# Latents projected by features, sums of squares by matmul, queries rotated on VectorE, and retention's chunks four slots apart

## The chip, the cores and the metric

The kernel runs on one core of a Trainium2 chip, as one program. The metric is the device time of one execution in microseconds. Where a text says TensorE, VectorE, ScalarE, GpSimd and SyncE, the profile writes PE (PEld for its weight loads), DVE, ACT, POOL and SP.

## The reference

A model of two layers on 1024 tokens of width 1024. Each layer projects `h` to 3,120 columns, runs four mixers on slices of them, joins them by `w_out`, and adds a feed-forward part. What the change touches, cut to it:

```python
(ssm_z, ssm_xbc, ssm_dt, mla_cq, mla_ckv, mla_kr, ret_q, ret_k, ret_v, ret_g,
 nsa_q, nsa_kc, nsa_vc, nsa_ks, nsa_vs, nsa_kw, nsa_vw, nsa_gate) = split_columns(h @ w_in[l])
y_b = mla(mla_cq, mla_ckv, mla_kr, ...)
# mla: latents of 256 and 128, a shared rope key of 32, 4 heads of 64 + 32
q = (rms_norm(c_q, q_norm_g) @ w_uq).reshape(bsz, S, H, 96)
q = concat([q_nope, apply_rope(q_pe, cos, sin)]) * 96 ** -0.5
kv = (rms_norm(c_kv, kv_norm_g) @ w_ukv).reshape(bsz, S, H, 64 + 64)
k = concat([k_nope, broadcast(apply_rope(k_rope, cos, sin))])
# rms_norm: x * rsqrt(mean(x * x) + 1e-5) * g;  apply_rope: [x1 cos - x2 sin, x1 sin + x2 cos]
# retention: chunks of 128 tokens, one after the other through a state
```

Everything is float32. The kernel gets this precision in the large products with pairs of a high and a low part and three matmuls for each product.

## The kernel before

Tokens are tiled by 128 (`NT` = 8 tiles). `hybrid_layers` calls for each layer `mixers`, `attention` and `dense`. In each of them every engine has its own program, written out by hand in order, and waits for the others by semaphores; `phase` ends a block with a barrier of all engines. SyncE issues all transfers. `ahead` is one tile with one semaphore through which a block's last act loads the first data of the next.

`mixers` projects the columns group by group (`projection_groups`, line 903). A group has its weights loaded by SyncE (`load`), split into a high part by ScalarE (`split_hi`, line 1286) and a low part by GpSimd (`low`, line 1085), one group ahead of its use. TensorE works by slots: a token group of n columns has 8 units, one for each tile, of 24 matmuls with the tile as weights and n columns moving (`tokens_unit`, lines 1115 to 1117). A group by features has 4 units, of 24 matmuls with 128 columns of the weights stationary and 512 tokens moving, each cut over two slots (`projected_features`, lines 1131 to 1133). ScalarE takes each unit from PSUM into `stage` (`take`, lines 1318 and 1320), and after each half of a group SyncE stores it to DRAM: `proj` and `tok` by tokens, `proj_T` by features (`store`). Between the slots TensorE gets the small matmuls of the state space (a chunk each 4 slots) and then of retention: chunk t starts at slot 33 + 5t of the 72, with parts j = 0 to 3 in four successive slots, and its output is scaled on VectorE at j = 4 (line 1593). VectorE rotates the chunk's queries and keys two slots ahead (`rotate`, lines 1548 to 1560). The groups after retention's are: two of 208 columns by tokens (cq, ckv, kr), nq and kc+vc+ks+kw of 256 by features, and vs+vw+gate of 140 by tokens. The block's end loads half of the latents.

`attention` has two blocks. The first (lines 1677 to 1878) makes the MLA queries, keys and values: TensorE turns a tile's latents (`turn`, line 1766), VectorE scales them by the gains into `cT` (`copy_c`, line 1844), TensorE projects them up (lines 1791 to 1793, fp32, two instructions a matmul), ScalarE squares the latents with an accumulator (`square`, lines 1805, 1806), VectorE and GpSimd make the root of the mean (lines 1836, 1752), and ScalarE and VectorE take the products scaled by it (`take`, lines 1811 and 1812; `values`, line 1853). GpSimd rotates queries and keys a half (4 tiles) at a time (`rotate`, lines 1734 to 1743). Then TensorE turns queries and keys tile by tile into the one buffer `pT` (`turn_qk`, lines 1774 and 1779), and ScalarE and VectorE split them into high and low parts (`highs`, `lows`, lines 1816 to 1860). The second block computes maxima, scores and sums.

## Time and profile before

| | us |
|---|---|
| time of three runs: lowest, median, highest | 3117.3, 3121.11, 3121.22 |
| the profiled execution | 3122.69 |
| its span in the trace | 3120.9 |
| TensorE busy in it | 2939.0 |

The profile is of one execution. The span is the time from its first to its last recorded instruction; the rest of the execution's time lies around it. Times in the rows are microseconds from the span's start, "mean ns" is nanoseconds. A timeline row reads: start, duration, engine, line, instruction, output <- inputs, and in brackets the idle time before it and what ended it. Matmuls overlap, so the distance between two starts is their price, not the duration of one. "x2" on a row means that so many instructions were merged in it.

### The profile page before, as it was taken

To read this page: it belongs to the slowest core of one execution; us is meant where nothing else is said; L and a number is where in the kernel's file an instruction comes from. 1 tells how busy PE (TensorE), PEld (TensorE's weight loads), DVE (VectorE), ACT (ScalarE), POOL (GpSimd) and SP (SyncE) were. 2 spreads that over 40 slices of the span, in tenths; PEclk is the share of its full clock that TensorE was granted. 3 is DMA by queue.
4 is the path that set the end of the run, shared out by engine and by line. 5 is a ranking of instruction groups with operands and counts; after the bars stand their busy time and mean duration, and the time that the engine had idled before them with its cause. 6 is when DMAs were issued, how large, how long until landed. Compare 5 with 4: busy or idle time off the path is not lost. (4 is left out here: it accounts for less than half of the span.)

```text
span 3120.9 us, 38057 instructions
## 1 busy us (share of the span) xinstructions
PE 2939.0 (94%) x15186; PEld 2372.2 (76%) x15186; DVE 1522.1 (49%) x2571; ACT 818.5 (26%) x1375; POOL 320.4 (10%) x284
## 2 busy tenths in 40 slices
PE   4999978999999999999979999799999999999997
PEld 4899855656878888888768998466567888888885
DVE  5554434354644444444645533434555444444456
ACT  3322132434221121122223221234342211112111
POOL 4121132000000000000221212320000000000003
PEclk9999987999999999999989999689999999999998
DMA  4123314103011111011121232321030110111111
GB/s 160 54 62 89 92 56 85 41 1 109 27 64 45 54 55 54 28 53 55 54 78 34 73 108 75 84 51 28 1 135 28 54 54 33 49 54 54 54 41 54
DMA packets 143190, 186.00 MB, mean 60 GB/s; under 512 B 29072, under 2 KB 118800, under 8 KB 143016
## 3 DMA queue, kind: packets, MB, share of 16 engines
q1 hardware_dynamic: 143016, 183.57, 19.2%
q8 instruction: 122, 2.00, 0.3%
q14 instruction: 52, 0.43, 0.0%
HBM read 153.83 MB, written 29.72 MB: 59 GB/s over the span
## 5 line engine op out<-in xcount | busy, mean ns | idle before, releaser
L691 PE MATMUL dense_acc<-mlp_w2hi,mlp_ahi 128*128 128x512 f32 x1024 | 400.3, 391 | 4.2 <-DVE mlp_alo L823 4.2
L387 PE MATMUL dense_tr<-x_hi,mlp_w1hi 128*128 128x512 f32 x1024 | 400.5, 391 | 3.8 <-PEq L474 3.8
L832 DVE TENSOR_TENSOR h<-h,dense_acc 128x512 f32<-128x512 f32 x448 | 302.1, 686 | 204.1 <-PE dense_acc L693 204.1
L389 PE MATMUL dense_tr<-x_hi,mlp_w1lo 128*128 128x512 f32 x1024 | 400.0, 391 | 0.0
L388 PE MATMUL dense_tr<-x_lo,mlp_w1hi 128*128 128x512 f32 x1024 | 399.9, 391 | 0.0
L693 PE MATMUL dense_acc<-mlp_w2hi,mlp_alo 128*128 128x512 f32 x1024 | 399.8, 390 | 0.0
L692 PE MATMUL dense_acc<-mlp_w2lo,mlp_ahi 128*128 128x512 f32 x1024 | 399.4, 390 | 0.0
L1115 PE MATMUL mix_acc<-mix_whi,x_hi 128*128 128x256 f32 (+3 forms) x1024 | 294.4, 287 | 13.4 <-DVE mix_wlo L1410 13.4
L817 DVE TENSOR_TENSOR mlp_square<-mlp_square 128x512 f32<-128x512 f32 x128 | 88.4, 692 | 440.4 <-ACT mlp_square L757 440.4
L1116 PE MATMUL mix_acc<-mix_wlo,x_hi 128*128 128x256 f32 (+3 forms) x1024 | 287.4, 281 | 0.0
L1117 PE MATMUL mix_acc<-mix_whi,x_lo 128*128 128x256 f32 (+3 forms) x1024 | 286.7, 280 | 0.0
L691 PEld LDWEIGHTS dense_acc<-mlp_w2hi,mlp_ahi 128*128 128x128 f32 x1024 | 193.1, 189 | 45.3 <-issue 5.4
L387 PEld LDWEIGHTS dense_tr<-x_hi,mlp_w1hi 128*128 128x128 f32 x1024 | 193.3, 189 | 44.2 <-issue 4.2
L2247 ACT ACTIVATE att_PT<-att_ST 128x512 f32<-128x512 f32 (+2 forms) x244 | 135.2, 555 | 340.3 <-PE att_ST L2140 205.5
L389 PEld LDWEIGHTS dense_tr<-x_hi,mlp_w1lo 128*128 128x128 f32 x1024 | 193.2, 189 | 40.2
L388 PEld LDWEIGHTS dense_tr<-x_lo,mlp_w1hi 128*128 128x128 f32 x1024 | 193.2, 189 | 40.1
L692 PEld LDWEIGHTS dense_acc<-mlp_w2lo,mlp_ahi 128*128 128x128 f32 x1024 | 193.1, 189 | 40.1
L693 PEld LDWEIGHTS dense_acc<-mlp_w2hi,mlp_alo 128*128 128x128 f32 x1024 | 192.8, 188 | 40.3
L1115 PEld LDWEIGHTS mix_acc<-mix_whi,x_hi 128*128 128x128 f32 x1024 | 196.5, 192 | 14.5 <-DVE mix_wlo L1410 14.2
L757 ACT ACTIVATE mlp_square<-dense_tr 128x512 f32<-128x512 f32 x128 | 76.3, 598 | 481.4 <-PE dense_tr L389 479.2
L749 ACT ACTIVATE mlp_w2hi<-mlp_raw 128x2048 fp32r<-128x2048 f32 x32 | 61.3, 1916 | 535.3 <-PE dense_acc L693 535.3
L1116 PEld LDWEIGHTS mix_acc<-mix_wlo,x_hi 128*128 128x128 f32 x1024 | 196.4, 192 | 0.1
(306 smaller groups left out, 5022.3 us busy)
## 6 DMA issues: line engine op xcount, KB each, us to landing
ahead<-w_mlp SPq DMA_DIRECT2D x32, 1024.0 KB
mlp_raw<-w_mlp SPq DMA_DIRECT2D x32, 1024.0 KB, 5.5
ahead<-w_in SPq DMA_DIRECT2D x18, 1024.0 KB, 5.6
residual<-h SPq DMA_DIRECT2D x16, 512.0 KB, 2.6
projections<-h SPq DMA_DIRECT2D x16, 512.0 KB, 4.1
mix_qkvg<-projections SPq DMA_DIRECT2D x16, 512.0 KB, 4.6
h<-residual SPq DMA_DIRECT2D x16, 512.0 KB, 4.7
att_raw_q<-projections_T SPq DMA_DIRECT2D x12, 512.0 KB, 8.7
```

Of the source, the lines that this page charges most:

```text
L387: pe.matmul(tr[:, n, :], wh, xh, start=(k == 0), stop=False)
L388: pe.matmul(tr[:, n, :], wh, xl, start=False, stop=False)
L389: mm = pe.matmul(tr[:, n, :], wl, xh, start=False, stop=(k == KT - 1))
L691: pe.matmul(out[:, m % 4, :], xh, wh, start=(begin and j == 0), stop=False)
L692: pe.matmul(out[:, m % 4, :], xh, wl, start=False, stop=False)
L693: mm = pe.matmul(out[:, m % 4, :], xl, wh, start=False, stop=(end and j == 1))
L817: dve.tensor_tensor(here, here, here, ALU.mult).then_inc(s.square_ready, 1)
L832: dve.tensor_tensor(part, part, out[:, m % 4, :], ALU.add).then_inc(s.down_added, 1)
L1115: pe.matmul(out, xh, whi[b][:, k, 0:n], start=(k == 0), stop=False)
L1116: pe.matmul(out, xh, wlo[b][:, k, 0:n], start=False, stop=False)
L1117: mm = pe.matmul(out, xl, whi[b][:, k, 0:n], start=False, stop=(k == KT - 1))
L2247: act.activation(PT[0:width, n % 3, c0:512], ST[0:width, n % 2, c0:512], ACT.Exp).then_inc(s.exp_ready, 1)
```

## The change

The rope key `kr` moves into the token group (now 172 columns, stored in `tok`), which comes first after retention's groups. The latents cq and ckv are projected by features and stored in `proj_T` (rows `ROW`); kc+vc joins ckv, and ks+kw is a group of its own, of 128 columns and 4 slots. Slots are listed in `places`, 68 instead of 72. Retention's chunks start every 4 slots, and a chunk's output is scaled at the first slot of the next. The block's end loads the first 512 tokens of the latents by features.

In the first block of `attention` the latents come turned, so TensorE's turns and their copies go. VectorE scales 512 tokens at a time, in SBUF. ScalarE squares without an accumulator, a half at a time, and TensorE sums the squares with matmuls against a column of ones, into a corner of `pT`. GpSimd takes one root for each half, makes the products of the keys' rotation once for all tiles before the first root, and rotates the keys. VectorE rotates the queries, a pair of tiles at a time. The turns of queries and keys follow three tiles behind the up-projections, in two buffers, instead of after them. `masks_in` lies in `v[1]`, and only the last column of `vm` is filled with ones. The second block reads its rows at their new places.

```diff
-TOK = 2 * HD + 3 * H
+TOKV = 2 * HD + 3 * H
+TOK = TOKV + ROPE
+
+ROW = dict(c=0, kv=3 * P, q=4 * P, k=4 * P + GW)
+ROWS = 4 * P + GW + P
...
-    half = (COL["rq"] - COL["cq"]) // 2
-    groups += [Group(half, [(COL["cq"] + half * i, half, 0)]) for i in range(2)]
-
-    groups += [Group(GW, [(COL["nq"], GW, 0)]), Group(GW, [(COL["kc"], P, 0), (COL["ks"], HD, P), (COL["kw"], HD, P + HD)])]
-    groups += [Group(TOK, [(COL["vs"], HD, 0), (COL["vw"], HD, HD), (COL["gate"], 3 * H, 2 * HD)])]
+    groups += [Group(TOK, [(COL["vs"], HD, 0), (COL["vw"], HD, HD), (COL["gate"], 3 * H, 2 * HD), (COL["kr"], ROPE, TOKV)])]
+
+    groups += [Group(QR, [(COL["cq"], QR, 0)]), Group(2 * P, [(COL["ckv"], KVR, 0), (COL["kc"], P, KVR)])]
+    groups += [Group(GW, [(COL["nq"], GW, 0)]), Group(P, [(COL["ks"], HD, 0), (COL["kw"], HD, HD)])]
...
-    SLOTS = UT + NT * (GN - GR)
-    GF = GN - 3
-    by_features = lambda g: GF <= g < GN - 1
-    SF, ST = UT + NT * (GF - GR), UT + NT * (GN - 1 - GR)
-    unit_of = lambda slot: slot if slot < SF else SF + (slot - SF) // 2 if slot < ST else slot - NT
-
-    S0, SSTEP, R0, RSTEP = UT + 1, 4, UT + 4 * NT + 1, 5
-    last_unit = [NT - 1] + [UX + 4 * i + 3 for i in range(3)] + [unit_of(UT + NT * i + NT - 1) for i in range(GN - GR)]
+    GT, GF = GR + 4, GR + 5
+    by_features = lambda g: g >= GF
+
+    places = [(g, j) for g in range(GR, GN) for j in range(NT if groups[g].width > P else NT // 2)]
+    slot_at = {place: UT + i for i, place in enumerate(places)}
+    SLOTS = UT + len(places)
+    ST = slot_at[GF, 0]
+    unit_of = lambda slot: slot if slot < ST else ST + (slot - ST) // 2
+
+    S0, SSTEP, R0, RSTEP = UT + 1, 4, UT + 4 * NT + 1, 4
...
-                load_first_latents(sp, ahead, proj)
+                sp.wait_ge(s.stored1, 16 * (GF + 1 - GR))
+                sp.wait_ge(s.stored0, 16 * (GF + 2 - GR))
+                load_latents(sp, ahead, proj_T)
...
+            pss = pT[:, 1, 1, 0, 0:2 * NT].rearrange("p (t i) -> p t i", i=2)
...
+                    sp.dma_start(c_raw[1], proj_T[ROW["c"]:ROW["c"] + 3 * P, 512:T].rearrange("(k p) t -> p k t", p=P)).then_inc(s.c_loaded, 16)
+                    sp.dma_start(rope[:], tab["t_rope_mla"]).then_inc(s.rope_loaded, 16)
+                    sp.dma_start(kr[:], tokens(tok, TOKV, TOK)).then_inc(s.rope_loaded, 16)
...
+                    def root(half):
                         ts = slice(HALF * half, HALF * (half + 1))
+                        pool.wait_ge(s.meaned, 2 * half + 2)
+                        pool.tensor_tensor(rr[:, ts, :], ss[:, ts, :], power[:], ALU.pow).then_inc(s.rooted, 1)
+                    def key_products():
+                        pool.wait_ge(s.rope_loaded, 32)
+                        cos, sin = rope[:, :, 0:HR].unsqueeze(2), rope[:, :, HR:ROPE].unsqueeze(2)
+                        a, b = kr[:, :, 0:HR].unsqueeze(2), kr[:, :, HR:ROPE].unsqueeze(2)
+                        pool.tensor_tensor(k1_[:], a, cos, ALU.mult)
+                        pool.tensor_tensor(k2_[:], b, sin, ALU.mult)
+                        pool.tensor_tensor(k3_[:], a, sin, ALU.mult)
+                        pool.tensor_tensor(k4_[:], b, cos, ALU.mult).then_inc(s.k_products, 1)
+                    def rotate_keys(half):
+                        ts = slice(HALF * half, HALF * (half + 1))
+                        pool.wait_ge(s.k_products, 1)
+                        all_heads = lambda t: t[:, ts, :, :].to_broadcast([P, HALF, H, HR])
+                        pool.tensor_tensor(kt[:, ts, :, NOPE:NOPE + HR], all_heads(k1_), all_heads(k2_), ALU.subtract).then_inc(s.k_rotated, 1)
+                        pool.tensor_tensor(kt[:, ts, :, NOPE + HR:QD], all_heads(k3_), all_heads(k4_), ALU.add).then_inc(s.k_rotated, 1)
+                    pool.memset(one[:], 1.0).then_inc(s.power_set, 1)
                     pool.memset(power[:], -0.5).then_inc(s.power_set, 1)
+                    pool.memset(vm[:, :, :, HD:HD + 1], 1.0).then_inc(s.filled, 1)
+                    pool.wait_ge(s.power_set, 2)
                     pool.wait_ge(s.filled, 1)
+                    key_products()
+                    root(0)
+                    rotate_keys(0)
+                    root(1)
+                    rotate_keys(1)
+                    pool.wait_ge(s.k_rotated, 4)
                     step(pool.memset(kh[QD:QD + H, :, :].bitcast(F32), 1.0))
...
+                    def sum_squares(half):
+                        pe.wait_ge(s.power_set, 2)
+                        pe.wait_ge(s.squared, 3 * half + 3)
+                        if half:
+                            pe.wait_ge(s.meaned, 2)
+                        for t in range(HALF * half, HALF * (half + 1)):
+                            for k in range(3):
+                                mm = pe.matmul(pss[:, t, k // 2:k // 2 + 1], sq[:, t, k * P:(k + 1) * P], one[:], start=(k != 1), stop=(k != 0),
+                                               skip_group_check=True)
+                        mm.then_inc(s.summed, 1)
+                    def up_project(t):
+                        pe.wait_ge(s.c_scaled, 3 * (t // HALF) + 3)
                         if t >= 2:
                             pe.wait_ge(s.q_out, t - 1)
                             pe.wait_ge(s.k_out, t - 1)
                             pe.wait_ge(s.v_out, t - 1)
+                        pe.matmul(pq(t), cT[:, 0, here(t)], wq[:, 0, :], start=True, stop=False)
+                        pe.matmul(pq(t), cT[:, 1, here(t)], wq[:, 1, :], start=False, stop=True)
+                        pe.matmul(up[:, 2 * (t % 2) + 1, :], cT[:, 2, here(t)], wkv[:], start=True, stop=True).then_inc(s.up_ready, 1)
+                    def turn(t):
+                        pe.wait_ge(s.q_rotated, t // 2 * 2 + 2)
+                        if t >= 2:
+                            pe.wait_ge(s.q_copied, t - 1)
+                        for h in range(H):
+                            mm = pe.transpose(pT[0:QD, t % 2, 0, h, :], qt[:, t, h, :], ident[:])
+                        mm.then_inc(s.q_turned, 1)
+                        pe.wait_ge(s.k_rotated, 2 * (t // HALF) + 2)
+                        pe.wait_ge(s.k_out, t + 1)
+                        if t == 1:
+                            pe.wait_ge(s.meaned, 4)
+                        if t >= 2:
+                            pe.wait_ge(s.k_copied, t - 1)
+                        for h in range(H):
+                            mm = pe.transpose(pT[0:QD, t % 2, 1, h, :], kt[:, t, h, :], ident[:])
+                        mm.then_inc(s.k_turned, 1)
+                    sum_squares(0)
+                    pe.wait_ge(s.weights_loaded, 32)
+                    for t in range(NT + LAG):
+                        if t < NT:
+                            up_project(t)
+                        if t == 1:
+                            sum_squares(1)
+                        if t >= LAG:
+                            turn(t - LAG)
...
+                    def square(half):
+                        for k in range(3):
+                            act.activation(sq[:, HALF * half:HALF * (half + 1), k * P:(k + 1) * P], c_raw[half][:, k, :].rearrange("p (t n) -> p t n", n=P),
+                                           ACT.Square).then_inc(s.squared, 1)
+                        act.wait_ge(s.rooted, t // HALF + 1)
+                        act.activation(q2[0:QD, :, here(t)], pT[0:QD, t % 2, 0, :, :], ACT.Copy, scale=float(QD ** -0.5)).then_inc(s.q_high, 1)
+                        act.activation(kh[0:QD, :, here(t)], pT[0:QD, t % 2, 1, :, :], ACT.Copy).then_inc(s.k_high, 1)
+                    act.wait_ge(ahead.sem, ahead.count)
+                    square(0)
+                    act.wait_ge(s.c_loaded, 16)
+                    square(1)
+                    for t in range(NT + LAG):
+                        if t < NT:
+                            take(t)
+                        if t >= LAG:
+                            highs(t - LAG)
...
+                    def scale(half):
+                            dve.tensor_scalar(cT[:, k, half_of(half)], c_raw[half][:, k, :], g, None, ALU.mult).then_inc(s.c_scaled, 1)
+                    def mean(half):
+                        ts = slice(HALF * half, HALF * (half + 1))
+                        dve.wait_ge(s.summed, half + 1)
+                        for i, n in enumerate((QR, KVR)):
+                            dve.tensor_scalar(ss[:, ts, i], pss[:, ts, i], 1.0 / n, EPS, ALU.mult, ALU.add).then_inc(s.meaned, 1)
+                        dve.wait_ge(s.rooted, t // HALF + 1)
+                    def rotate(pair):
+                        ts = slice(2 * pair, 2 * pair + 2)
+                        dve.wait_ge(s.q_out, 2 * pair + 2)
+                        if pair:
+                            dve.wait_ge(s.q_rotated, 2 * pair)
+                        else:
+                            dve.wait_ge(s.rope_loaded, 32)
+                        cos = rope[:, ts, 0:HR].unsqueeze(2).to_broadcast([P, 2, H, HR])
+                        sin = rope[:, ts, HR:ROPE].unsqueeze(2).to_broadcast([P, 2, H, HR])
+                        a, b = qt[:, ts, :, NOPE:NOPE + HR], qt[:, ts, :, NOPE + HR:QD]
+                        dve.tensor_tensor(p1[:], a, cos, ALU.mult)
+                        dve.tensor_tensor(p2[:], b, sin, ALU.mult)
+                        dve.tensor_tensor(p3[:], a, sin, ALU.mult)
+                        dve.tensor_tensor(p4[:], b, cos, ALU.mult).then_inc(s.q_products, 1)
+                        dve.wait_ge(s.q_products, pair + 1)
+                        dve.tensor_tensor(a, p1[:], p2[:], ALU.subtract).then_inc(s.q_rotated, 1)
+                        dve.tensor_tensor(b, p3[:], p4[:], ALU.add).then_inc(s.q_rotated, 1)
+                        dve.scalar_tensor_tensor(q1[0:QD, :, here(t)], pT[0:QD, t % 2, 0, :, :], QD ** -0.5, q2[0:QD, :, here(t)].bitcast(F32),
+                        dve.tensor_tensor(kl[:, :, here(t)], pT[0:QD, t % 2, 1, :, :], kh[0:QD, :, here(t)].bitcast(F32),
+                    dve.wait_ge(ahead.sem, ahead.count)
+                    scale(0)
+                    mean(0)
+                    dve.wait_ge(s.c_loaded, 16)
+                    scale(1)
+                    for t in range(NT + LAG):
+                        if t < NT:
+                            values(t)
+                            if t == 0:
+                                mean(1)
+                            if t % 2:
+                                rotate(t // 2)
+                        if t >= LAG:
+                            lows(t - LAG)
```

## Rows read from the trace of the kernel before

**Rows 1.** Page, part 1: busy time, share of the span, instructions
```profile
PE 2939.0 (94%) x15186; PEld 2372.2 (76%) x15186; DVE 1522.1 (49%) x2571; ACT 818.5 (26%) x1375; POOL 320.4 (10%) x284
```

**Rows 2.** Windows: stretch, length, engines' busy, PEclk (granted), DMA share, GB/s
```profile
149.20:405.30 256.10, 249.65 (x1983) 238.13 (x1981) 122.17 (x269) 62.85 (x137) 44.95 (x23) 1.00 0.26 75
405.30:462.80 57.50, 35.38 (x137) 22.04 (x137) 23.52 (x69) 22.74 (x65) 26.16 (x40) 0.79 0.17 54
462.80:492.80 30.00, 25.30 (x76) 17.54 (x77) 15.86 (x29) 1.75 (x4) 4.18 (x12) 0.50 0.73 158
1943.00:2001.90 58.90, 36.23 (x137) 22.38 (x137) 23.39 (x69) 22.64 (x65) 26.19 (x40) 0.74 0.17 52
417.90:437.50 19.60, 15.75 (x56) 8.54 (x54) 8.64 (x35) 10.04 (x34) 8.94 (x16) 1.00 0.00 1
452.00:492.60 40.60, 31.62 (x105) 21.84 (x104) 21.35 (x37) 6.50 (x12) 4.53 (x13) 0.50 0.54 116
```

**Rows 3.** Timeline of ScalarE in `mixers`, layer 0: start, duration, instruction
```profile
97.35 0.60 ACT L1299 ACTIVATE mix_xT<-mix_acc 128x512 f32<-128x512 f32 x1 [4.17 <-PE mix_acc L1146]
...
102.79 0.60 ACT L1299 ACTIVATE mix_xT<-mix_acc 128x512 f32<-128x512 f32 x1 [4.18 <-PE mix_acc L1146]
...
291.39 0.35 ACT L1320 ACTIVATE h<-mix_acc 128x208 f32<-128x208 f32 x1 [3.23 <-PE mix_acc L1117]
294.07 0.34 ACT L1320 ACTIVATE h<-mix_acc 128x208 f32<-128x208 f32 x1 [2.33 <-PE mix_acc L1117]
...
391.94 0.29 ACT L1320 ACTIVATE h<-mix_acc 128x140 f32<-128x140 f32 x1 [3.29 <-PE mix_acc L1117]
394.62 0.29 ACT L1320 ACTIVATE h<-mix_acc 128x140 f32<-128x140 f32 x1 [2.40 <-PE mix_acc L1117]
```

**Rows 4.** Timeline of TensorE in `attention`, layer 0
```profile
414.81 1.65 PE L1791 MATMUL att_up<-att_wq,att_cT 128*128 128x384 f32 x2 [2.80 <-DMA att_wkv<-w_ukv]
...
418.62 0.49 PE L1766 MATMUL att_pc<-ident,ahead 128*128 128x128 f32 x3
...
421.42 0.81 PE L1791 MATMUL att_up<-att_wq,att_cT 128*128 128x384 f32 x2
...
423.57 0.49 PE L1766 MATMUL att_pc<-ident,att_lat 128*128 128x128 f32 x3
...
438.75 1.09 PE L1774 MATMUL att_pT<-ident,att_qt 128*96 128x128 f32 x4 [5.10 <-POOL att_kt L1743]
...
453.56 1.06 PE L1774 MATMUL att_pT<-ident,att_qt 128*96 128x128 f32 x4 [0.81 <-DVE att_q L1857]
...
462.77 0.44 PE L2114 MATMUL att_S<-att_kh,att_q 96*128 96x128 f32 x1 [2.19 <-PEq L127]
```

**Rows 5.** Timeline of ScalarE, same stretch
```profile
418.82 0.58 ACT L1811 ACTIVATE att_qt<-att_up,att_rr 128x384 f32<-128x384 f32 x1 [6.18 <-PE att_up L1793]
```

**Rows 6.** Timeline of VectorE, same stretch
```profile
461.24 0.69 DVE L1860 TENSOR_TENSOR att_kl<-att_pT,att_kh 96x512 fp32r<-96x512 f32 x1 [0.17 <-ACT att_kh L1818]
```

**Rows 7.** Timeline of GpSimd, same stretch
```profile
409.80 0.10 POOL L1745 MEMSET att_power<- 128x2 f32 x1 [1.99 <-POOLq L127]
...
434.68 0.34 POOL L1734 TENSOR_TENSOR att_t<-ahead,att_rope 128x64 f32<-128x64 f32 x1
```

**Rows 8.** VectorE's groups by line and shape: count, busy, mean ns, idle
```profile
L1548 DVE TENSOR_TENSOR mix_t<-mix_qkvg,mix_rope 128x256 f32<-128x256 f32 x16 | 6.7, 417 | 0.0
```

**Rows 9.** Timeline of all engines, layer 0, a weight split on GpSimd
```profile
157.33 5.00 POOL L1085 TENSOR_TENSOR mix_wlo<-ahead,mix_whi 128x2048 fp32r<-128x2048 f32 x1 [17.20 <-ACT mix_whi L1286]
...
157.82 4.80 DVE L1483 TENSOR_TENSOR mix_xdt<-mix_xb,mix_dt 128x256 f32<-128x256 f32 x1
```

**Rows 10.** DMA issues: count, KB each, us to landing; last row from 403:425
```profile
att_raw_t<-projections_tok SPq DMA_DIRECT2D x2, 560.0 KB, 15.6
...
ahead<-w_in SPq DMA_DIRECT2D x2, 48.0 KB, 4.8
...
att_lat<-projections SPq DMA_DIRECT2D x1, 832.0 KB, 5.3
```

200 lines of the change are left out of this document (48 added, 152 removed).

## The prediction

> **What bounds the kernel now.** I read the page's busy shares first: TensorE is busy for 94% of the span [rows 1], so a change pays only where it shortens TensorE's own work or closes a hole in it. Then the windows by stage [rows 2], which show where the holes are. In a layer the diff touches two places: the projection of `mixers`, which is unbroken TensorE work at full clock, and the first block of `attention`, 405.3 to 462.8 us in layer 0 and 1943.0 to 2001.9 in layer 1, where TensorE is busy for 35 of 58 us and VectorE, ScalarE and GpSimd for less than half. In that block a chain through the engines sets the time, not one engine. Last the timelines of the single engines, for the pace of a projection unit [rows 3] and for the links of that chain [rows 4 to 7].
>
> **Part 1, projection columns.** A unit is always 24 matmuls (8 k by three passes), so the distance between two ScalarE takes with no inserted work between them, divided by 24, is the price of one. Rows 3: 208 columns 294.07-291.39 = 2.68 us, 140 columns 394.62-391.94 = 2.68 us, 512 columns (weights stationary, tokens moving) 102.79-97.35 = 5.44 us. So 140 and 208 columns cost the same 0.112 us a matmul: below some width the columns are free. 512 columns cost 0.227.
> Before: two groups of 208, 8 units each, 16 x 2.68 = 42.9; two groups by features, 4 units each, 8 x 5.44 = 43.5; the token group of 140, 8 x 2.68 = 21.4. Sum 107.8.
> After: the token group of 172, between 140 and 208 and so again 8 x 2.68 = 21.4; cq, ckv+kc and nq by features, 12 x 5.44 = 65.3; ks+kw, 2 units, 10.9. Sum 97.6.
> TensorE saves **10.2 us a layer**. It is all on the path: rows 2 show TensorE busy in 249.7 of 256.1 us there. A take by features (0.60 us for 512 columns) stays far below a unit.
>
> **Part 2, retention four slots apart.** The instructions are the same, only closer: 8 chunks end at slot 64 of 68 instead of at the last of 72. I cost it at nothing. What hides it: a chunk has four slots of 2.7 us and about 3 us of inserted matmuls, 14 us; VectorE needs for a chunk some 19 instructions of at most 0.42 us [rows 8], 8 us. One thing could add: the group's weight split on GpSimd now always falls near a rotation. The trace shows such a meeting: VectorE's product of 157.82 took 4.80 us instead of 0.42, ending with GpSimd's split that began at 157.33 [rows 9]. The rotation has two slots of slack after it, so I take 0, bounds 0 and 4 us a layer. `retention_out` now comes at the next chunk's first slot, before the matmul that overwrites its bank, so no new wait on TensorE; and the retention tail after the last projection (VectorE, GpSimd) moves under the last units. Nothing is gained by that, as the next item shows.
>
> **Part 3, the seam.** The next block begins at 409.80 [rows 7] after the last unit's take; its store and the load of the latents are issued only after that take, in both versions. The last take now moves 512 columns (0.60 us against 0.29 [rows 3]) and the store is 512 KB, not 280. I charge **0.4 us a layer** (bounds 0 and 1.5). The latents' load lands, as before, about 1 us after the block begins.
>
> **Part 4, the first block of attention.** B is the block's begin, 409.80; the second block's first matmul is at 462.77 = B+53.0 [rows 4, 7]. The old chain has holes: TensorE waits for the half-wise rotation on GpSimd, 5.10 us before 438.75 [rows 4], and then turns one tile per round trip through ScalarE and VectorE, because there is one buffer of turned tiles. The new block, step by step:
> - Latents are there at about B+1.1. Three squares of 512 columns at about 0.5 us end at B+2.7. The sum of squares of a half is 12 fp32 matmuls of one column, two instructions each. No such operation is in the trace; the nearest row is a turn, four in 1.06 us at half clock [rows 4], 0.21 us apart, so 24 x 0.21 = 5.1 us, B+7.9 (at full clock 2.6). The clock is at half here: the instruction pair of 414.81 takes 1.65 us where that of 421.42 takes 0.81 [rows 4].
> - up_project(0) at half clock is 418.62-414.81 = 3.8 us, (1) at full 423.57-421.42 = 2.15: B+13.7. Weights are there at B+5 (414.81 in rows 4), so that wait is covered.
> - Squares of half 1 want the second load. The old second load landed 5.3 us after its issue [rows 10], B+7.6, so they end at B+9.2. sum_squares(1), full clock, 2.6: **B+16.3**.
> - Beside it GpSimd: the key rotation waits for the rope table and for kr, then 4 products, each between the 64-element row of 0.34 us [rows 7] and twice that, 2 us, then root(0), 1 us by estimate, since a small GpSimd instruction here is a third of a microsecond and a power is dearer. kr is 1024 pieces of 128 bytes. The rows have two loads of 1024 short pieces: 4.8 us (48 bytes each) and 15.6 us (560 bytes each, among 2 MB of other loads) [rows 10]. Issued at about B+4 it lands at B+8.8 to B+19.6. I take B+9, the first, as here as there little is queued behind it; then root(0) is at B+12, the first take at B+12, v_out(0) at B+13.6, before TensorE wants it at 16.3. So up to B+11.7 a late kr costs nothing, beyond that it costs one for one.
> - Then a steady run. For a tile TensorE has 2.15 of up_project and 8 transposes of a turn, 1.0 at full clock: 3.15. ScalarE has 0.58 and less for the two copies of a take [rows 5], together 1.0, and about 1.05 for the highs: 2.0. VectorE has values 0.4, two lows of 0.6 [rows 6], and half of a pair's rotation: 6 instructions of 128 elements, at most the 256-element row's 0.42 each [rows 8], estimate 0.25, so 0.8 a tile: 2.4, at the upper bound 2.9. TensorE remains the bound. Six up_projects and four turns from B+16.3 are 6 x 2.15 + 4 x 1.0 = 16.9: B+33.2.
> - The tail: take and values of tile 7, 1.6, rotation of the last pair 1.7, lows of tiles 4 to 7 at 1.2 each, 4.8, small waits 0.5: B+41.8. From the last lows' end (461.24+0.69) to the next block's matmul was 0.85: **B+42.6**.
> Instead of B+53.0: **10.4 us a layer** saved. Bounds: 15 (sums at full clock, VectorE's pieces at their short end), and 2.7 (kr at B+19.6, which is 7.7 later).
> On this block two rules of the Trainium skill. Its page "SBUF — State Buffer" (SBUF: two separate sides) says that VectorE and GpSimd hold a common port pair exclusively, and that a VectorE instruction with two SBUF inputs meets only GpSimd instructions that read SBUF. Rows 9 agree. By it the memsets beside the rotation cost nothing and the two GpSimd rotations of keys and the casts at most their own length, under 3 us, most of it while VectorE waits. "DMA: Bandwidth & Descriptors" (Specifications) says that pieces under 512 bytes miss line rate; that speaks against kr, and is the second rival, whose price stands on rows 10.
>
> **The second block** (462.8 to 492.8) runs at half clock, mean 0.50 [rows 2], with TensorE busy in 25 of 30 us. Its work is not touched. I take it as it is: the seam before it is again a TensorE hole, 2.19 us in the row of 462.77 [rows 4], after turns that fill only half of the time.
>
> **Sum.** A layer: 10.2 + 10.4 - 0.4 = 20.2; layer 1 shows the same block and the same 58.9 us [rows 2]; two layers 40.4. The profiled execution took 3122.69 us (span 3120.9), so 3082.3; the runs' median is 1.6 below that execution: 3080.7. Rounded, **3081 us**.
>
> **Rivals.**
> 1. The clock stays at 2.4 GHz into the second block. For: the new block keeps TensorE denser; in the old one it was at full clock at mean 1.00 from 417.9 on [rows 2]. Against: the fall at 452.0 came with turns only, as the new tail has. TensorE's 25.3 us of work in those 30 would be 12.7, but VectorE alone has 15.9 there and waits for TensorE's results between; I take half of the 14 us that remain above VectorE's own work, 7 a layer: 3067.
> 2. kr lands late, B+19.6, and with it every take: TensorE starts its run at B+23.9 and not 16.3, 7.7 a layer: 3096. For: 128-byte pieces queued behind 1.5 MB. Against: the 48-byte load.
> 3. VectorE becomes the bound of the run, because the rotation of the queries came from GpSimd to it: at 0.42 an instruction plus a lock now and then, 3.5 us a tile instead of 3.15, 3 us a layer: 3087. It lies in the forecast's own range.
> 4. The edit does in the first block not what it is said to: the one-column matmuls do not bring the clock up, and it stays at half in the whole block. Then 2.7 + 2 x 5.1 + 8 x 3.8 + 8 x 1.7 + 2.6 = B+59.5, 6.5 more than before: the two layers save 2 x (10.2-6.5-0.4) = 6.6 us: 3114.
> 5. The other side: as 4, and the clock does not come up at the start of the second block's dense run either. Rows 2 show that this can be: 452.0 to 492.6 at 0.50, with TensorE busy in 31.6 of 40.6 us. Each microsecond of TensorE work past the old point of rise costs half of itself; from 6.6 us of work a layer on, the change is a loss. With 20 us it is 10 a layer lost: 3114+20 = 3134, slower. Against: up_projects brought the clock up at 417.9, 3 us after their first.
>
> **How the numbers follow.** Forecast 0.64 (own range 3070 to 3091, from the bounds of parts 2 to 4), with rival 3 in it; rival 1 0.14; rival 2 0.13; rival 4 0.04; rival 5 0.05. The range reaches over rivals 1 and 2: 3064 to 3098; what is left out is 4, 5 and the ends of the others, some 0.18. About 0.2% (6 us) is what a measurement of this kernel can tell from no change. Faster 0.91, within 0.2% 0.04, slower 0.05.
>
> **What would show it.** Right: no rows of 208 columns; 512-column units at 5.44 us; from the first projection unit after the state-space stage to the last take 10 us less; the second block's first matmul 42 to 43 us after the first block's begin; TensorE without a hole between the second sum and the last up_project. Wrong: TensorE waiting for `att_rr` or ScalarE's take before up_project(2) (kr late); a granted clock of 0.50 between B+12 and B+33; TensorE waiting for retention's `mix_qk` in the projection stage; holes before the turns that VectorE ends. The prediction falls if the block takes more than 50 us or the projection stage saves less than 7.

## The result, and the profile after

The changed kernel takes **3080.8 us** (median of 4 runs, 3077.2 to 3081.2) beside 3121.2 of before (4 runs): ratio 0.9864, 95% interval 0.9845 to 0.9883. Forecast were 3081 us and a range of 3064 to 3098. On another chip the same two kernels stood at 3087.7 and 3122.6, ratio 0.9887 (0.9869 to 0.9905). Ratios leave disturbed runs out and can differ in the last digit from the quotient of the medians.

The profiled execution took 3077.2 us (span 3075.3), 45.5 less than before's. Page, part 1; TensorE has 28.5 us less work than in [rows 1]:

```profile
PE 2910.5 (95%) x14754; PEld 2338.2 (76%) x14754; DVE 1534.8 (50%) x2559; ACT 806.0 (26%) x1303; POOL 295.9 (10%) x242
```

The windows of after, columns as in [rows 2]. The stretches are: in layer 0 from the first projection unit narrower than 256 columns to the last projection matmul's end ("the stage"), from there to the next block's begin ("the seam"), the first block of `attention`, and the first 30 us of the second; in layer 1 the stage, the first block, and everything from the second block to the end.

```profile
269.34:395.46 126.12, 123.87 (x755) 105.88 (x753) 60.50 (x152) 26.64 (x53) 24.86 (x13) 1.00 0.31 94
395.46:400.90 5.44, 0.00 (x0) 0.00 (x0) 0.00 (x0) 0.60 (x1) 0.00 (x0) 0.85 0.67 188
400.90:443.23 42.33, 34.67 (x161) 24.29 (x161) 21.77 (x58) 19.03 (x38) 12.40 (x17) 0.86 0.19 55
443.23:473.23 30.00, 25.30 (x83) 17.47 (x84) 16.74 (x31) 1.93 (x5) 4.20 (x12) 0.54 0.72 157
1790.65:1915.51 124.86, 123.78 (x755) 105.89 (x753) 60.61 (x152) 26.57 (x53) 24.88 (x13) 1.00 0.31 95
1920.79:1964.34 43.55, 35.88 (x160) 24.84 (x161) 21.86 (x58) 19.03 (x38) 12.49 (x17) 0.83 0.18 53
1964.34:3075.35 1111.01, 1070.59 (x4909) 827.74 (x4909) 554.62 (x846) 276.06 (x411) 56.41 (x62) 0.97 0.17 53
```

The same stretches of before (without the 30 us, which stand in [rows 2]):

```profile
270.83:404.27 133.44, 132.41 (x989) 121.54 (x987) 52.66 (x147) 28.69 (x62) 23.08 (x12) 1.00 0.32 90
404.27:409.80 5.53, 0.89 (x9) 0.75 (x7) 1.86 (x5) 0.70 (x2) 1.01 (x1) 0.81 0.74 199
409.80:462.77 52.97, 35.35 (x137) 22.01 (x137) 21.76 (x64) 22.33 (x64) 25.12 (x38) 0.79 0.11 38
1808.87:1941.92 133.05, 132.42 (x989) 121.56 (x987) 50.58 (x147) 28.64 (x62) 23.06 (x12) 1.00 0.32 90
1947.44:2001.83 54.39, 36.16 (x136) 22.31 (x137) 21.68 (x64) 22.22 (x64) 25.12 (x38) 0.75 0.11 36
2001.83:3120.91 1119.08, 1079.84 (x4909) 834.35 (x4909) 555.03 (x846) 276.62 (x411) 56.48 (x62) 0.97 0.17 52
```

Read one above the other they give the account: stages 7.3 and 8.2 us shorter, seams the same, first blocks 10.6 and 10.8, and 8.1 in the untouched part behind layer 1's first block, where TensorE has the same 4909 matmuls in 9.2 us less busy time. The rest (1.5 us before the first stage, and 1.3 lost between the layers' changed parts) is not the change.

TensorE in the first block of layer 0, timeline (start, duration, instruction, idle before):

```profile
404.14 5.25 PE L1783 MATMUL att_pT<-att_one,att_qt 128*128 128x1 f32 x24 [8.68 <-ACT att_qt L1828]
409.25 1.63 PE L1793 MATMUL att_up<-att_wq,att_cT 128*128 128x384 f32 x2
...
413.27 0.81 PE L1793 MATMUL att_up<-att_wq,att_cT 128*128 128x384 f32 x2
...
415.42 2.73 PE L1783 MATMUL att_pT<-att_one,att_qt 128*128 128x1 f32 x24
418.01 0.89 PE L1793 MATMUL att_up<-att_wq,att_cT 128*128 128x384 f32 x2
...
425.42 0.60 PE L1802 MATMUL att_pT<-ident,att_qt 128*96 128x128 f32 x4
...
428.44 0.60 PE L1802 MATMUL att_pT<-ident,att_qt 128*96 128x128 f32 x4
...
434.49 0.60 PE L1802 MATMUL att_pT<-ident,att_qt 128*96 128x128 f32 x4
...
438.33 0.61 PE L1802 MATMUL att_pT<-ident,att_qt 128*96 128x128 f32 x4 [1.93 <-DVE att_q L1895]
...
443.23 0.30 PE L2152 MATMUL att_S<-att_kh,att_q 96*128 96x128 f32 x1 [2.49 <-PEq L131]
```

GpSimd there:

```profile
400.90 0.10 POOL L1757 MEMSET att_one<- 128x1 f32 x1 [8.32 <-POOLq L131]
...
410.66 0.49 POOL L1745 TENSOR_TENSOR att_kp<-att_kr,att_rope 128x128 f32<-128x128 f32 x1 [9.53 <-DMA att_kr<-projections_tok]
...
412.37 1.64 POOL L1737 TENSOR_TENSOR att_rr<-att_ss,att_power 128x8 f32<-128x8 f32 x1
...
421.57 3.51 POOL L1768 MEMSET att_kh<- 4x4096 f32 x1
425.15 0.61 POOL L1770 CAST att_masks<-att_v 128x512 fp32r<-128x512 f32 x1
```

ScalarE, in layer 0's last projections and the block:

```profile
284.12 0.31 ACT L1325 ACTIVATE h<-mix_acc 128x172 f32<-128x172 f32 x1 [3.50 <-PE mix_acc L1122]
286.80 0.31 ACT L1325 ACTIVATE h<-mix_acc 128x172 f32<-128x172 f32 x1 [2.06 <-PE mix_acc L1122]
...
389.94 0.60 ACT L1323 ACTIVATE h<-mix_acc 128x512 f32<-128x512 f32 x1 [5.99 <-PE mix_acc L1138]
395.49 0.60 ACT L1323 ACTIVATE h<-mix_acc 128x512 f32<-128x512 f32 x1 [4.65 <-PE mix_acc L1138]
402.32 1.67 ACT L1828 ACTIVATE att_qt<-ahead 128x512 f32<-128x512 f32 x3 [6.23 <-DMA ahead<-projections_T]
...
414.10 0.58 ACT L1834 ACTIVATE att_qt<-att_up,att_rr 128x384 f32<-128x384 f32 x1 [2.90 <-POOL att_rr L1737]
```

VectorE in the block: a rotation's first and last instruction (six in all, of which four like the first), and the last of the lows:

```profile
424.08 0.28 DVE L1885 TENSOR_TENSOR att_qp<-att_qt,att_rope 128x128 f32<-128x128 f32 x1
...
425.21 0.70 DVE L1891 TENSOR_TENSOR att_qt<-att_qp 128x128 f32<-128x128 f32 x1
...
441.69 0.68 DVE L1898 TENSOR_TENSOR att_kl<-att_pT,att_kh 96x512 fp32r<-96x512 f32 x1
```

DMA issues of the seam (count, KB, us from issue to landing):

```profile
att_c_rest<-projections_T SPq DMA_DIRECT2D x1, 768.0 KB, 6.5
...
att_rope<-t_rope_mla SPq DMA_DIRECT2D x1, 128.0 KB, 5.8
att_kr<-projections_tok SPq DMA_DIRECT2D x1, 128.0 KB, 6.5
```

### The profile page after: what moved, and what is told of

It reads as the page before. It is cut to its first block and busy times, and to the rows that moved or that the text cites. A ratio compares the mean times of both kernels' runs of the same rounds, so it can differ in the third digit from the quotient of the medians.

```text
span 3075.3 us, 37031 instructions
## 1 busy us (share of the span) xinstructions
PE 2910.5 (95%) x14754; PEld 2338.2 (76%) x14754; DVE 1534.8 (50%) x2559; ACT 806.0 (26%) x1303; POOL 295.9 (10%) x242
## 5 line engine op out<-in xcount | busy, mean ns | idle before, releaser
L1120 PE MATMUL mix_acc<-mix_whi,x_hi 128*128 128x256 f32 (+2 forms) x768 | 223.1, 291 | 13.6 <-DVE mix_wlo L1416 13.6
L692 PEld LDWEIGHTS dense_acc<-mlp_w2hi,mlp_ahi 128*128 128x128 f32 x1024 | 192.9, 188 | 45.2 <-issue 5.4
L1121 PE MATMUL mix_acc<-mix_wlo,x_hi 128*128 128x256 f32 (+2 forms) x768 | 217.5, 283 | 0.0
L1122 PE MATMUL mix_acc<-mix_whi,x_lo 128*128 128x256 f32 (+2 forms) x768 | 217.0, 283 | 0.0
L436 POOL TENSOR_TENSOR norm_rstd<-norm_var,norm_power 128x1 f32<-128x1 f32 x32 | 30.6, 957 | 1586.7 <-DVE norm_var L403 1586.7
L1120 PEld LDWEIGHTS mix_acc<-mix_whi,x_hi 128*128 128x128 f32 x768 | 148.0, 193 | 14.3 <-DVE mix_wlo L1416 14.2
```

The source lines that it names most:

```text
L692: pe.matmul(out[:, m % 4, :], xh, wh, start=(begin and j == 0), stop=False)
L1120: pe.matmul(out, xh, whi[b][:, k, 0:n], start=(k == 0), stop=False)
L1121: pe.matmul(out, xh, wlo[b][:, k, 0:n], start=False, stop=False)
L1122: mm = pe.matmul(out, xl, whi[b][:, k, 0:n], start=False, stop=(k == KT - 1))
```

## The experiments

Twelve kernels ran, on three chips. What decides is the table of stretches, read from each trace in the same way (us; a "+" marks a stage with a long stretch of half clock in it):

| kernel | stage, layer 0 | stage, layer 1 | first block, layer 0 | first block, layer 1 | from there to the end |
|---|---|---|---|---|---|
| before | 133.4 | 133.1 | 53.0 | 54.4 | 1119.1 |
| before_again | 134.1 | 133.1 | 54.9 | 55.0 | 1113.5 |
| step_alone | 137.9 | 135.2 | 54.7 | 55.3 | 1113.4 |
| mixers_alone | 136.9+ | 125.6 | 53.9 | 54.6 | 1119.2 |
| attention_alone | 133.9 | 132.9 | 42.2 | 42.6 | 1111.0 |
| after | 126.1 | 124.9 | 42.3 | 43.5 | 1111.0 |
| after_again | 126.6 | 125.0 | 42.9 | 42.7 | 1116.4 |
| retention_five | 124.4 | 138.5+ | 41.4 | 41.0 | 1113.4 |
| root_first | 137.3+ | 125.4 | 42.5 | 43.2 | 1110.8 |
| warm_root | 136.3+ | 127.8 | 40.0 | 41.2 | 1117.0 |
| early_all | 136.3+ | 124.8 | 41.2 | 41.3 | 1113.5 |
| turns_after | 136.7+ | 125.0 | 44.2 | 44.7 | 1119.4 |
| gpsimd_pairs | 136.3+ | 124.9 | 45.2 | 45.6 | 1114.9 |
| early_warm | 128.3 | 141.0+ | 41.2 | 41.4 | 1111.1 |

The seam is 5.3 to 5.6 us, but 5.0 to 5.1 in early_all, in early_warm and in layer 1 of step_alone, 9.0 in retention_five, and 5.6 to 5.7 in warm_root, whose extra matmuls lie in it.

### The two halves of the change apart

**mixers_alone** (the diff shows the block's source of latents; the block itself is that of before):

```diff
-    rows = tokens(proj, COL["cq"], COL["cq"] + LAT)
+    rows = tokens(proj, COL["rq"], COL["rq"] + LAT)
```

Expected: 

> The changed kernel's mixers (projection columns, retention four slots apart) with the first block of attention as it was before; its latents are loaded, in the same shape and bytes, from columns of the projections that hold rotated queries, so the values are not the reference's. Theory (from the two traces, block begin to block begin: 7.4 us less in layer 0, 8.4 in layer 1): 3121.2 - 15.8 = 3105. The record's own split (9.8 us per layer) would give 3101.5. Rival, that the shorter way to the second block in the profile (1.3 and 6.4 us there) comes with these stages: 3097.

Measured: 3123.6 us (11 runs, 3107.6 to 3133.5) beside 3126.5: ratio 0.9988 (0.9972 to 1.0004), an interval that holds 1. No theory had this. The trace says where it went:

```profile
275.06:411.92 136.86, 133.59 (x755) 115.65 (x753) 60.25 (x152) 26.66 (x53) 24.83 (x13) 0.93 0.29 86
286.92:307.40 20.48, 20.48 (x99) 20.48 (x97) 7.11 (x19) 2.15 (x6) 4.07 (x2) 0.50 0.17 44
```

Layer 1's stage is 7.5 us shorter than before's (table), as in after. Layer 0's, the first window, has the 755 matmuls of after's, but over the 20.5 us of the second the granted clock is 0.50, that is 1.2 GHz, although TensorE is busy for all of them; the stage is 10.2 us longer than that of after_again. Its cause is taken up below.

**attention_alone**:

```diff
-TOK = 2 * HD + 3 * H
+TOKV = TOK = 2 * HD + 3 * H
+ROW = dict(c=0)
-                load_first_latents(sp, ahead, proj)
+                load_latents(sp, ahead, proj_T)
```

and the first block of after. Expected: 

> The mixers of before with the changed first block of attention (sums of squares on TensorE, queries rotated by VectorE in pairs, turns three tiles behind, two buffers for the turned tiles); its latents by features and its key part are loaded in the same shape from rows and columns that hold other projections, so the values are not the reference's. Theory (record: 10.4 us per layer; traces: 10.65 and 10.8): 3121.2 - 21.4 = 3100. Rival, that the second block's 7.7 us come with this block, since TensorE enters the second block after denser work: 3092. Rival, that the block gains only because kr and the latents are there early: over 3105.

Measured: 3093.7 beside 3126.5, ratio 0.9897 (0.9884 to 0.9911): 33 us, more than the block's own 2 x 11.8, as the first rival had it. The block is 42.2 and 42.6 us, and from there to the end 1111.0. Much of what comes on top of the block lies behind it: the half clock with which a second block starts ends 21.7 and 22.1 us after its begin, where the eight second blocks behind an old first block have it until 27.2 to 30.3. So the two halves give 33 and 3 us, not the 21 and 20 of the record.

### Retention's spacing

**retention_five**: `RSTEP` is 5 again in the changed kernel.

```diff
-    S0, SSTEP, R0, RSTEP = UT + 1, 4, UT + 4 * NT + 1, 4
+    S0, SSTEP, R0, RSTEP = UT + 1, 4, UT + 4 * NT + 1, 5
```

Expected: 

> The changed kernel with retention's chunks five slots apart, as before: there are 68 slots, so the last chunk starts at slot 68 and nothing lies beside it. Theory: part 2 is what lets retention end inside the stage, and undoing it lays one chunk's own chain (8 us of VectorE work and its hand-overs, 8 to 14 us) bare behind the last projection, at a TensorE clock that may be half: 3081 + 2 x 8 to 14 = 3097 to 3109. Rival (only the waits within chunks matter, 1.5 us per layer in the trace): 3078 to 3084.

Measured: 3092.7 us, ratio 0.9892 (0.9877 to 0.9907); the changed kernel's was 0.9887 on another chip. My theory fell. The windows of layer 0's stage and seam:

```profile
274.81:399.17 124.36, 122.49 (x733) 105.44 (x732) 49.16 (x140) 25.51 (x49) 22.66 (x11) 0.99 0.33 95
399.17:408.14 8.97, 2.90 (x24) 2.21 (x22) 4.21 (x12) 2.11 (x5) 2.05 (x4) 0.87 0.50 146
```

The bare tail costs 3.5 us in the seam (9.0 against 5.4), since the last store's landing hides the rest of it, and the stage gives 1.8 to 2.3 back, since 22 of its matmuls now lie behind it; the block is 0.9 to 1.5 shorter as well. Stage, seam and block of layer 0 are together 174.7 us, where after has 173.9 and after_again 174.9. In the changed kernel part 2 is worth nothing that these traces can tell.

**step_alone**: the kernel before with `RSTEP = 4` and `retention_out` where the change has it.

```diff
-    S0, SSTEP, R0, RSTEP = UT + 1, 4, UT + 4 * NT + 1, 5
+    S0, SSTEP, R0, RSTEP = UT + 1, 4, UT + 4 * NT + 1, 4
```

Expected: 

> The kernel before with only retention's chunks four slots apart (72 slots, so eleven slots less of retention beside the last projections). Theory: the projections bind, the stage keeps its 133.4 us and the seam its 5.5 us, whatever the spacing: 0 +- 1.5 us, ratio 1.000. Rival, the wait of TensorE for ScalarE's copy of the turned tile (2.2 us against 0.7 us in the first traces) grows with the denser chunks: 1 to 2 us per layer slower. Rival (Theory B of the half-clock stretch lies in the spacing): 5 to 10 us slower, with the stretch in the trace.

Measured: 3134.6 beside 3123.2, ratio 1.0030 (1.0019 to 1.0040): slower, by the first rival's mechanism. Waits of TensorE in layer 0's stage (us in total, times, longest):

```profile
PE mix_rowsp L1226 <- ACT mix_qkT L1346: 4.4, 3, 2.3
```

against this of before_again:

```profile
PE mix_rowsp L1226 <- ACT mix_qkT L1346: 1.5, 1, 1.5
```

The wait is 2.9 of layer 0's 3.8 us; the last chunk's eight matmuls, formerly in the seam, are 1.1. The three waits stand 10.7, 38.9 and 69.1 us into the stage, one for each group of eight slots: at four slots every second chunk starts where a group's weights are split on ScalarE, ahead of the chunk's copy. Layer 1's stage is 2.1 longer. So the stages show 5.9 us of the 8.9 by which the profiled execution is longer than before_again's. The rest (2.3 before the first stage, 1.2 between the layers) lies where the edit changes nothing.

### Whose is the half clock in the projections?

**before_again** and **after_again** are the two kernels unchanged. Expected: 

> The changed kernel unchanged, beside runs of before on the same chip. The first set of comparisons has stretches of half clock in layer 0's and layer 1's projections (20.5 us at 298 in two runs, 34 us at 1816 in one) that neither first trace has. Theory A, these stretches belong to this chip and hit before as well: ratio 0.986 to 0.988. Theory B, the changed mixers bring them: ratio 0.990, 3090 to 3095, and such a stretch in the trace.

> The kernel before, unchanged, with a trace of its own on this chip. Open is why the changed mixers alone gave 3 us where their stages are 7 to 8 us shorter per layer in the trace: five of eight traces with them have a 20.5 us stretch of half clock at the end of layer 0's projections (10 us longer stage), none of the two traces with the mixers of before. Theory A, the stretch is the chip's and meets both: ratio 1.000, and traces of before's mixers show it too (stage 143 us instead of 133.4). Theory B, the changed mixers bring it: stage 133 to 134 us here.

Measured: after_again 3087.7 (6 runs, 3080.1 to 3094.5), ratio 0.9887; before_again 1.0001 (0.9986 to 1.0017), which is also the resolution of such a comparison. Neither trace has a long stretch of half clock in a stage. Over all fourteen the count is 0 of 4 with the old columns and 8 of 10 with the new, 20.5 us in layer 0 (six) and 34 and 31 us in layer 1 (retention_five, early_warm). All begin 11 to 12 us after the stage does. Step_alone, with retention at four slots and the old columns, has none, and retention_five, with the new columns at five slots, has one, so the spacing alone does not bring it. What is there is a hole. ScalarE in mixers_alone, layer 0:

```profile
283.78 1.91 ACT L1294 ACTIVATE mix_whi<-ahead 128x2048 fp32r<-128x2048 f32 x1 [1.90 <-DMA ahead<-w_in]
285.60 0.58 ACT L1354 ACTIVATE mix_qkT<-mix_trp 128x512 f32<-128x512 f32 x1
```

and TensorE:

```profile
281.37 0.60 PE L1222 MATMUL mix_trp<-ident,mix_qk 128*128 128x128 f32 x4
...
286.23 0.37 PE L1234 MATMUL mix_rowsp<-mix_qkT 64*128 64x128 f32 x1 [1.60 <-ACT mix_qkT L1354]
```

Retention's first turned tile is ready at 282, but in ScalarE's program the split of the next group's weights stands ahead of its copy, and that split waits for the weights' load. So TensorE waits for a DMA by way of ScalarE, and the clock falls at 286.92, 0.7 us behind the wait. ScalarE in before, at the same place:

```profile
278.94 1.60 ACT L1286 ACTIVATE mix_whi<-ahead 128x1664 fp32r<-128x1664 f32 x1 [1.25 <-DMA ahead<-w_in]
280.44 0.58 ACT L1346 ACTIVATE mix_qkT<-mix_trp 128x512 f32<-128x512 f32 x1
```

There the next group has 208 columns: a split of 1.60 us instead of 1.91 and a smaller load, and TensorE's hole is 0.65 us. Over the 28 stages of all traces this hole is below 1.3 us in 16, none of them with a fall at that point, and 1.3 us or more in 12: eight have the long stretch (1.31, 1.34, 1.46, 1.60, 1.67, 1.78, 1.79, 2.61), three a short one of 3.4 us (1.52, 1.87, 2.09), one none (before_again, 1.52). The size of the hole does not decide alone: three later holes in the stages, 1.35 (after_again), 1.42 (root_first) and 2.25 us (step_alone), have no fall behind them. But the new columns lengthen this first hole, in layer 0 from 1.08 us in the mean of four to 1.53 in the mean of ten, and in layer 1 from at most 0.4 to 0.84 to 2.61. So theory B fits, with a mechanism that the traces suggest and no experiment has isolated. The kernel that would test it, the copy ahead of the split on ScalarE, was not run.

### The order inside the new block

**root_first**, one look ahead on a small gate:

```diff
-                    key_products()
                     root(0)
+                    key_products()
                     rotate_keys(0)
```

Expected: 

> GpSimd takes the root of the first half's sums ahead of the four products for the keys. The trace of after has the products from 410.66 (kr landing) to 412.4 and the root to 414.0; sums are there at 409.4. Theory: the first take (414.10) then waits for up(0), whose end is 413.27 because TensorE is at half clock: 0.8 us per layer, 3079. Rival (the root is the gate of the whole block, 2.4 us per layer): 3076. Rival (keys come late for the first turns): 3081 or more.

Measured: ratio 0.9883 (0.9866 to 0.9899), first blocks 42.5 and 43.2: nothing gained. With B the block's begin, the first take moves from B+13.2 to B+12.8, but up_project(2) starts at B+17.3, in after at B+17.1. TensorE sets it: at its half-clock pace up_project(0), up(0) for short, gives way to up(1) at B+12.6 only, and up(1) and the second sum follow without a hole. So kr, which landed at B+9.8, was no gate.

**turns_after** (one trace):

```diff
-            LAG = 3
+            LAG = NT
```

Expected: 

> All turns of queries and keys stand behind the last up-projection on TensorE, ScalarE and VectorE (LAG is 8 instead of 3), as they nearly did before. Theory: the interleaving is worth what the tail then costs: up-projections run at 1.9 to 2.2 us per tile (to about B+29), then eight turns at the pace of VectorE's two lows and ScalarE's two takes, 1.4 to 2.0 us each, to B+29+13 to 16: the second block begins at B+43 to B+46 instead of B+42.3. Rival, the interleaving carries most of the 10.6 us: B+50 or later.

Measured: first blocks 44.2 and 44.7, so the interleaving is worth 1.5 to 2 us of some 11.8; the theory held. The rest of the gain I put down to what the block no longer does: 24 transposes and 24 copies of latents, the per-tile roots, the wait for rotations by halves (5.10 us in [rows 4]) and one buffer's round trips. No run separates these.

**gpsimd_pairs** (one trace), with `rotate` itself moved word for word:

```diff
-                            if t % 2:
-                                rotate(t // 2)
...
+                    rotate(0)
                     step(pool.memset(kh[QD:QD + H, :, :].bitcast(F32), 1.0))
+                    rotate(1)
...
+                    rotate(2)
+                    rotate(3)
```

Expected: 

> The queries' rotation, still in pairs of tiles, done by GpSimd instead of VectorE. Theory: six instructions of 0.45 us make 2.7 us per pair where the cadence gives 6.05, so only the last pair shows, 1.4 us later than VectorE's 1.3: the second block begins at B+43.5 to B+44.5 instead of B+42.3. Rival, GpSimd's instructions and VectorE's hold each other up as in retention (5.00 beside 4.80 us there): 3 to 6 us per layer. Rival, who rotates is all the same: B+42.3.

Measured: 45.2 and 45.6, 2.5 to 2.9 us a layer beside the mean of 42.7, a little above the theory, but not where the theory had it. TensorE's first turn of the queries waits for GpSimd, where the second root and the second half of the keys stand ahead of the first pair:

```profile
440.77 0.64 PE L1828 MATMUL att_pT<-ident,att_qt 128*96 128x128 f32 x4 [1.73 <-POOL att_qt L1775]
```

In after that turn waits for nothing (422.39). So the step from up(3) to up(4) takes 4.95 us instead of 3.02, in both layers. The last pair on GpSimd, first and last row:

```profile
454.01 0.46 POOL L1769 TENSOR_TENSOR att_qp<-att_qt,att_rope 128x128 f32<-128x128 f32 x1 [3.17 <-ACT att_qt L1860]
...
456.21 0.45 POOL L1775 TENSOR_TENSOR att_qt<-att_qp 128x128 f32<-128x128 f32 x1
```

It takes 2.65 us where VectorE takes 1.4, and yet nothing is lost there: from the start of the last up_project to the second block it is 10.6 us in both layers, in after 10.9. VectorE, free of the rotation, is that much ahead with its lows. So the theory's number came from the wrong place: the loss is at the first pair and not at the last.

### Towards a better version

**warm_root**, with root_first's order:

```diff
+                spare = bank_of(unit_of(SLOTS - 1) + 1)
+                for i in range(20):
+                    pe.matmul(spare[:], whi[GN - 1][:, i % KT, 0:P], hi[:, i % KT, 0:512], start=True, stop=True)
...
+                    for i in range(12):
+                        pe.transpose(up[:, 3, 0:P], ident[:], ident[:])
                     sum_squares(0)
```

Expected: 

> Root ahead of the key products, and TensorE kept busy over the seam by matmuls whose results nobody reads (20 of 512 columns behind the last projection, 12 small ones at the block's begin). Theory: the clock stays full, sums of squares(0) take 2.6 us instead of 5.25 and up(0) 2.1 instead of 4.0, the first take moves from B+13.2 to about B+10.4 (the squares of the second half stand before it on ScalarE), the second block begins 3 to 3.6 us earlier per layer: about 3074 beside after's 3081. Rival, the full clock is paid back by an earlier or longer half-clock stretch in the second block: same as after within 3 us. Rival, a landing (c_rest B+8.6, weights) holds it: 1 us per layer.

Measured: 3085.9, ratio 0.9886 (0.9857 to 0.9916), the same as after_again. In the trace the block is 1.5 to 2.9 us shorter and the seam 0.3 longer, 1.2 to 2.6 us a layer, less than the 3 to 3.6 of the theory: the first sum takes 3.57 us in layer 1, the clock falling in its course, and up(0) begins at half clock, its pair at 1943.88 taking 1.63 us. The timing does not show even that much.

**early_all**, with root_first's order:

```diff
+                    if unit == SLOTS - 2:
+                        load_latents(sp, nc, ahead, proj_T, tok, tab, w)   # c, kr, rope, gains
```

Expected: 

> The key part, the rotation table and the gains are loaded ahead with the first half of the latents, two slots before the projections end; the second half is the block's first load; root before the key products. Theory: squares(0) begin 1.3 us earlier, the root no longer stands behind kr, and the first take follows up(0), which TensorE still does at half clock: B+11.5 to B+12 instead of B+13.2, so 1.3 to 2 us per layer, 3077 beside after's 3081. Rival 2 of the record (kr is the gate): 2 to 2.5 us per layer as well, but then the first take moves with the root. Rival, the weights land last: no gain, 3081.

Measured: 3079.4 (6 runs), ratio 0.9870 (0.9847 to 0.9892), beside after_again's 0.9887 in the same comparison; the intervals overlap. In the traces block and seam are 46.2 and 46.4 us against 48.3 and 48.0, about the range foreseen. Its six executions fall into two groups, four of 3071.8 to 3080.6 us at a mean granted clock of 0.972 and two of 3091 at 0.967; the traced one, with the long stretch, is of the second. It is the one version that may be better, by 4 us; a measurement has not shown it.

**early_warm**, the edits of early_all and of warm_root together:

```diff
-                for i in range(20):
+                for i in range(10):
...
-                    for i in range(12):
+                    for i in range(14):
```

Expected: 

> The early loads, the root ahead of the key products and the busy TensorE over the seam together (10 matmuls of 512 columns behind the last projection, since 20 of them ended 2 us after the block could have begun, and 14 small ones at the block's begin). Theory: sums of squares(0) B+1.8 to B+4.5 at full clock, up(0) from the weights' landing B+6.5 to B+8.7 (early_all: B+11.2), first take B+8.8; the second block begins 2.5 us per layer before early_all's 41.2 us: B+38.7; 3072 to 3075 where after_again has 3081 to 3087. Rival, the clock falls to half anyway at the block's begin: B+41. Rival, the half-clock stretch of the second block starts earlier and eats it: seam and block shorter, the total the same.

(The 2 us in it was a misreading of mine; the 20 matmuls delay the block by 0.3.)

Measured: 3092.1, ratio 0.9886 (0.9864 to 0.9907), block 41.2 and 41.4: no better than early_all. TensorE in layer 0:

```profile
408.60 1.72 PE L1822 MATMUL att_up<-ident 128*128 128x128 f32 x14 [2.84 <-PEq L131]
410.67 2.81 PE L1790 MATMUL att_pT<-att_one,att_qt 128*128 128x1 f32 x24 [0.35 <-ACT att_qt L1837]
414.97 1.65 PE L1800 MATMUL att_up<-att_wq,att_cT 128*128 128x384 f32 x2 [1.49 <-DMA att_wkv<-w_ukv]
```

The sum runs at full clock (2.81 us), then TensorE waits 1.49 us for the weights, and the first up_project is at half clock again (1.65 against the 0.81 of after's row of 413.27). The clock fell at 413.47, as that wait began; the seam's own 2.84 us of idle time stand before the small matmuls. The half-clock stretch was not removed but moved behind the sum and is 6.8 us long, in after 13.7; a landing became the gate. Both rivals on the block held in part.

## Why the prediction was right, point by point

- **Part 1, projection columns, 10.2 us a layer.** The mechanism is right: 172 columns take 286.80-284.12 = 2.68 us a unit, like 140 and 208. The units by features take 395.49-389.94 = 5.55 us, not the 5.44 of [rows 3], which came from another stage: 108.7-99.1 = 9.6. The stage shrinks by 7.4 (layer 0) and 7.9 (layer 1), means of the traces with the spacing of their own kernel and no half clock in the stage, because the next point takes about 2 of it. The record's line for falling was 7; the first pair's layer 0 has 7.3.
- **Part 2, 0 (bounds 0 and 4).** Costed too low, within its bounds: TensorE waits for ScalarE's copy, 2.2 us in layer 0 of after against 0.7 before (4.4 in step_alone), and the last chunk's matmuls (1.1 us) come from the seam into the stage. I had seen that the weight split would now always fall on a chunk, but looked for the price in GpSimd's half of it and not in ScalarE's. TensorE waiting for retention in the stage was one of the record's own signs of being wrong, and it was there, though small.
- **Part 3, the seam, +0.4.** 5.4 us before and after: 0.
- **Part 4, 10.4 us.** Milestones of layer 0, forecast and found (B = 400.90): first sum begins B+2.7, +3.2, and takes 5.1, 5.25; up(0) begins +7.9, +8.35; second sum ends +16.3, +17.1; a tile of the run 3.15, 3.02; turns of tile 4 begin after the last up_project at +33.2, +33.6; last lows end +41.8, +41.5; second block +42.6, +42.3. VectorE's 0.25 was 0.28, and root(0), an estimate of 1, was 1.64 us, both under cover; the old trace had a power of 128x2 elements at 0.70 us, which would have been a nearer row than the products. In the record's working, 7.9 + 3.8 + 2.15 is B+13.85, not B+13.7, and rival 2's delay comes out as 7.6 or 7.9 a layer by its own rows, not 7.7. The forecast's starting point was one trace: its 53.0 is the lowest of eight old blocks, whose mean is 54.5; against the six of the unchanged new block, mean 42.7, the gain is 11.8.
- **kr (rival 2).** It landed 6.5 us after its issue, the rope table's equal bytes in 5.8. The Trainium skill's page "DMA: Bandwidth & Descriptors" (Specifications) says that pieces below 512 bytes miss line rate; 0.7 us is all that this trace shows for pieces of 128 bytes. The rival fell, and root_first shows that even the 0.7 was not on the path.
- **The lock (rival 3).** Beside the 3.51 us memset of 421.57 VectorE's rotation instructions take their 0.28 us, and the one that meets the cast of 425.15 takes 0.70. The Trainium skill's page "SBUF — State Buffer" (SBUF: two separate sides) would have it so, since a memset reads no SBUF; the trace agrees. VectorE was not the bound, since a tile took 3.02.
- **The second block, 0.** Not right. The half clock at its start ended 27.7 us after its begin instead of 30.3, its first 30 us have 0.54 granted, and behind layer 1's first block there are 8.1 us less in the first pair of traces. Over all traces the gain is smaller: 1113.9 mean of ten (1110.8 to 1119.4) against 1116.3 of four (1113.4 to 1119.2); the ranges overlap. The half clock itself is clearer: it ends 27.2 to 30.3 us after the begin in all eight second blocks behind an old first block, and at 21.2 to 23.4 in 11 of the 20 behind a new one. This is a small form of rival 1.
- **What no step held**: the projections' own clock. A stretch of 20.5 us takes 10 us from the execution that it meets, and I had let the stage run at mean 1.00 because one trace did. It is what is left to explain why the mixers alone are worth 3 us in the timing where their clean stages are 15.3 shorter. The granted clock of every timed execution fits: its mean is 0.9622 over the 11 of mixers_alone and 0.9661 over the 15 of before beside them. With the two levels of 1.2 and 2.4 GHz this is 2 x (1 - 0.9622) x 3122 = 236 us at half clock against 212. Those 24 us more cost some 12, by this estimate, which is what is missing between 15.3 and 3. Where in an execution they lie, only the traces tell.
- **The sum, 40.4.** Measured 40.4 and, on the second chip, 34.9. From the means, stages and seams 2 x 7.8, blocks 2 x 11.8, the rest 2.5 and, between the layers, 1.8: 43.5 us without half clock in a stage. That 40.4 came out exactly is luck: parts 1 to 3 were together too high by 2 a layer, part 4 too low by 1.4, the second block was left out, and one more loss was unknown. Rivals 4 and 5 fell: the clock was full from B+12.0 on in layer 0 and from B+14.4 in layer 1.

## What to carry to other kernels

Look at what stands ahead of each hand-over in its engine's program, a wait for a load above all: behind a hole of 1.3 us in TensorE's work 10 us were lost in clock. Measure the halves of a change apart, and take a stretch from more than one trace before calling it a baseline. A gate that ends latest by the profile is worth moving only if the engine behind it would then be free.

## What the runs showed of the hardware that I had not expected

- Behind a single hole of 1.3 to 2.6 us in work that was otherwise unbroken, the clock went to half for 20.5 to 34 us in 8 of 12 cases, with TensorE busy all the while in mixers_alone (20.48 of 20.48 us). Behind three later holes of 1.35 to 2.25 us it did not.
- In early_warm, with dummy work on both sides of the seam, the clock was full through the first sum and fell at 413.47, as a hole of 1.49 us began; the seam's 2.84 us of idle time lie before the block's first matmul at 408.60.
- GpSimd's power of 128x8 elements takes 1.64 us and of 128x2 in before 0.70, where a product of 128x128 takes 0.46.
